# Five weight slots at a stride of 8224 bytes in place of 8192, on a three-part transformer stack

## The reference

```python
def swiglu(h, w_gu, w_down):
    gate, up = jnp.split(h @ w_gu, 2, axis=-1)      # 1024 -> 2 x 2816
    return (jax.nn.silu(gate) * up) @ w_down        # 2816 -> 1024

x = x + 0.5 * swiglu(rms_norm(x, ffn1_norm[l]), ffn1_w_gu[l], ffn1_w_down[l])
h = rms_norm(x, mix_norm[l]) @ a_w_in[i]
...
x = x + jnp.concatenate([o_a, o_m], axis=-1) @ w_out[l]
x = x + 0.5 * swiglu(rms_norm(x, ffn2_norm[l]), ffn2_w_gu[l], ffn2_w_down[l])
```

## Time and profile before

| | |
|---|---|
| median of 3 runs | 2920.57 us (2917.97 to 2921.03) |
| span of the profiled execution | 2913.7 us |
| TensorE busy | 2827.3 us, 97% |
| VectorE busy | 1796.8 us, 62% |
| ScalarE busy | 1492.0 us, 51% |
| DMA | 489.12 MB, mean 168 GB/s |

### The profile page before, as it was taken

One profiled execution on the slowest core, in us unless ns is written; L12 is line 12 of the kernel. 1 busy time (PEld: TensorE's weight loads), 2 busy tenths in 40 slices (PEclk: granted clock), 3 DMA queues, 4 the chain that ended last, 5 costly groups with the idle time before them and its releaser, 6 DMA issues. The chain is left out here.

```text
span 2913.7 us, 47309 instructions
## 1 busy us (share of the span) xinstructions
PE 2827.3 (97%) x20443; PEld 2624.9 (90%) x20443; DVE 1796.8 (62%) x2467; ACT 1492.0 (51%) x2011; POOL 26.5 (1%) x41
## 2 busy tenths in 40 slices
PE   8999999999998999999999999999999999999999
PEld 7998978999986999999998988989999899998898
DVE  5557756566566656555678655566556655656655
ACT  6447435455455545443575634454454544544643
POOL 1000000000000000000001000000000000000000
PEclk9999999999999999999999999999999999999999
DMA  6555115555552556555452455555555555554553
GB/s 231 184 175 162 52 44 186 187 166 181 188 161 87 179 188 203 190 188 171 138 182 92 145 169 194 188 173 188 188 177 176 170 188 187 182 189 150 196 189 129
DMA packets 370110, 489.12 MB, mean 168 GB/s; under 512 B 15424, under 2 KB 329186, under 8 KB 369776
## 3 DMA queue, kind: packets, MB, share of 16 engines
q1 hardware_dynamic: 368944, 485.90, 51.9%
q0 software_dynamic: 640, 0.20, 0.0%
q10 hardware_dynamic: 320, 0.01, 0.0%
HBM read 485.02 MB, written 1.05 MB: 167 GB/s over the span
## 5 line engine op out<-in xcount | busy, mean ns | idle before, releaser
L873 PE MATMUL work<-input_hi,weights_hi 128*128 128x256 f32 x3424 | 959.5, 280 | 1.8 <-DVE weights_lo L241 1.7
L876 PE MATMUL work<-input_hi,weights_lo 128*128 128x256 f32 x3424 | 956.2, 279 | 0.0
L875 PE MATMUL work<-input_lo,weights_hi 128*128 128x256 f32 x3424 | 955.9, 279 | 0.0
L231 DVE TENSOR_TENSOR weights_lo<-weights_raw,weights_hi 128x2048 fp32r<-128x2048 f32 (+2 forms) x282 | 629.5, 2235 | 320.1 <-ACT weights_hi L211 319.6
L873 PEld LDWEIGHTS work<-input_hi,weights_hi 128*128 128x128 f32 x3424 | 643.6, 188 | 6.8 <-DVE weights_lo L241 2.1
L875 PEld LDWEIGHTS work<-input_lo,weights_hi 128*128 128x128 f32 x3424 | 643.5, 188 | 4.4
L876 PEld LDWEIGHTS work<-input_hi,weights_lo 128*128 128x128 f32 x3424 | 643.5, 188 | 0.0
L215 ACT ACTIVATE weights_hi<-weights_raw,params 128x512 fp32r<-128x512 f32 (+2 forms) x736 | 462.0, 701 | 329.7 <-DMA weights_raw<-in_ffn_w_in 164.0
L211 ACT ACTIVATE weights_hi<-weights_raw 128x2048 fp32r<-128x2048 f32 (+2 forms) x282 | 524.0, 1864 | 169.3 <-DMA weights_raw<-in_ffn_w_up 101.1
L241 DVE SCALAR_TENSOR_TENSOR weights_lo<-weights_raw,params,weights_hi 128x512 fp32r<-128x512 f32 (+2 forms) x736 | 492.6, 733 | 168.6 <-ACT weights_hi L215 168.5
L334 PE MATMUL acc<-weights_hi,hidden_hi 128*128 128x512 f32 x880 | 349.6, 397 | 7.5 <-DVE hidden_lo L1049 5.7
(11 more groups left out here) (565 smaller groups left out, 3462.3 us busy)
## 6 DMA issues: line engine op xcount, KB each, us to landing
weights_raw<-in_ffn_w_gu SPq DMA_DIRECT2D x176, 512.0 KB, 4.7
weights_raw<-in_ffn_w_in SPq DMA_DIRECT2D x176, 512.0 KB, 4.7
weights_raw<-in_ffn_w_down SPq DMA_DIRECT2D x66, 1024.0 KB, 4.9
weights_raw<-in_w_in SPq DMA_DIRECT2D x44, 1024.0 KB, 5.3
weights_raw<-in_ffn_w_out SPq DMA_DIRECT2D x44, 1024.0 KB, 4.9
weights_raw<-in_a_w_in SPq DMA_DIRECT2D x29, 1024.0 KB, 5.5
weights_raw<-in_ffn_w_gate SPq DMA_DIRECT2D x44, 512.0 KB, 3.9
weights_raw<-in_ffn_w_up SPq DMA_DIRECT2D x44, 512.0 KB, 5.0
```

Source lines behind the costliest of these rows:

```text
L231: last = self.nc.vector.tensor_tensor(self.wl[:, n % SLOTS, 0:kc * cols], raw, self.wh[:, n % SLOTS, 0:kc * cols].bitcast(F32), ALU.subtract)
L873: nc.tensor.matmul(o, wh[:, k, ms], K.hi[:, c, :], start=(c == 0 and m == 0), stop=False, skip_group_check=True)
L875: nc.tensor.matmul(o, wh[:, k, ms], K.lo[:, c, :], start=False, stop=False, skip_group_check=True)
L876: last = nc.tensor.matmul(o, wl[:, k, ms], K.hi[:, c, :], start=False, stop=(c == DC - 1), skip_group_check=True)
```

## The change

The slots of the three weight tiles are laid 2056 elements (8224 bytes) apart in place of 2048 (8192 bytes). An item still fills at most 2048 elements of its slot; the last 32 bytes of each slot are not used. `weights_lo` and `weights_hi` grow by 160 bytes each, so `weights_hi` begins 160 bytes later, and every tile behind it 320 bytes later. No instruction is added, removed or moved, and no shape, wait or count is changed.

```diff
@@ -20,6 +20,7 @@
 SLOT = 2048
+STRIDE = SLOT + 8
 SLOTS = 5
@@ -97,9 +98,9 @@
-        self.wl = self.sb("weights_lo", [P, SLOTS, SLOT], F32R)
-        self.raw = nc.alloc_sbuf_tensor_at("weights_raw", [P, SLOTS, SLOT], F32, offset=nc.sbuf_base - SLOTS * SLOT * 4)
-        self.wh = self.sb("weights_hi", [P, SLOTS, SLOT], F32R)
+        self.wl = self.sb("weights_lo", [P, SLOTS, STRIDE], F32R)
+        self.raw = nc.alloc_sbuf_tensor_at("weights_raw", [P, SLOTS, STRIDE], F32, offset=nc.sbuf_base - SLOTS * STRIDE * 4)
+        self.wh = self.sb("weights_hi", [P, SLOTS, STRIDE], F32R)
```

## The result

The changed kernel takes 2927.08 us (median of 11 runs, 2924.39 to 2932.76) against 2917.97 us for the kernel before, measured with it: a ratio of 1.0033, 95% interval 1.0024 to 1.0041. It is slower by a third of a percent: 9.1 us between the two medians, 9.6 us by the ratio. The forecast was 2924 us on a median of 2920.57, slower by 0.1%, with slower as the likeliest of the three signs (0.41).

The account below looks back on a forecast made before the run. TensorE's distance between matmul starts was taken to bound the kernel. Input +6.7 us and hidden -4.0 us sum to +2.7 us on the median of 2920.57, so 2924 us; range 2895 to 2950, the forecast's own 2909 to 2939.

Parts of the forecast that it names:

- The bound: Whole kernel: TensorE, busy 2827.3 of 2913.7 us, sets the time through the distance between starts of two matmuls.
- That addresses count: All matmuls: the streamed operand's start behind the stationary one, modulo 512, sets the distance, 113.4 to 119.9 ns at 256 columns.
- The rival of no effect: All matmuls: addresses don't matter and nothing changes, 2920.6 us; chance 0.20.
- Input, +6.7 us: 13344 matmuls streaming input past weights: mean distance rises from 116.8 to 117.3 ns; bounds -45 to +41 us.
- The signs of being right: Feed-forward stretches: equal counts and waits, distances of 114 to 119 ns repeating every five items, slot 0 quickest, 1 and 2 slowest.
- the pattern is broken: Input matmuls: remainders differing within each group of three slow them, 118.7 ns and 2946 us or 119.9 and 2962; chance 0.18.
- Hidden, -4.0 us: 2640 matmuls of 512 columns, weights past hidden: 231.0 ns, 1.5 ns less each; bounds -14 to +2 us.
- What was left at nothing: Some 2,600 remaining matmuls on weights, rounding, splitting and loads: no change taken.
- The rival that was faster: Matmuls on input and hidden: spreading the slots frees TensorE of collisions, -59 us, 2862 us, or half way 2891; chance 0.13.

Follow-up runs that it names:

- experiments 1 and 2: Kernel before plus a 160-byte gap: first behind weights_hi, 2885.54 us, ratio 0.9896; second ahead of all tiles, 2919.18 us, ratio 1.0005.
- The scans: Kernel before with slots 8224 bytes apart, gaps keeping both weight tiles at equal remainders, input 32 or 192 behind slot 0: single executions 2923.86 and 2924.86 us.
- experiment 5: Kernel before with slots kept at 8192 bytes, 40 unused words ahead of weights_hi and 40 behind it: 2926.64 us, ratio 1.0031.
- experiment 7: in192 plus a gap in each feed-forward placing the hidden tiles at 0 modulo 256 behind the slots: 2903.6 us, ratio 0.9954 to the kernel before.
- in192: Kernel before plus a 160-byte gap behind weights_hi, slots still 8192 bytes apart, input 192 behind both weight tiles: 2885.54 us, ratio 0.9896.
- hid64: in192 plus a gap in each feed-forward placing the hidden tiles at 192 modulo 256 behind the slots: 2878.0 us, ratio 0.9879 to the kernel before.

## Why the prediction was right, and where it was not

**The bound** held. TensorE's start distances set the time; the rest moved by less than 3 us (under "The sum").

**That addresses count** was told as a reading and not as shown. It is shown now: experiments 1 and 2 change one thing each, and the one that moves no tile against another changes nothing. The rival of no effect (0.20) is out. The rule of the Trainium skill's page SBUF — State Buffer, section "Who interferes with whom", that PE never waits on anyone, is about one engine holding up another; as the prediction took it, to say that the place of the operands costs nothing, it does not hold: 113.4 to 120.0 ns for matmuls of one form decide.

**Input, +6.7 us.** The sign was right, the size too small: 118.1 less 116.8 ns on 13344 matmuls is +18 us. Two steps of the pricing were off.

The larger one is the price for what no row had modulo 512. For remainders that are 224, 96, 64, 32 and 0 modulo 256 the prediction took the mean of its six rows, 117.6 ns. The scans show 118.3, 119.9, about 117.5, about 117 and 119.8 ns. It had a row at 352, which is 96 modulo 256, of 119.9 ns, and did not use it because the roles were the other way round; the scans show that this makes no difference. With the measured prices, and still each matmul by its own remainder, slots 0 to 4 come to 115.6, 118.4, 118.1, 119.9 and 117.8 ns, a mean of 117.95: +15 us.

The smaller one is to price each matmul by its own remainder and to average over a group of three. It gave slot 0 as the quickest at 114.8 ns; measured are 117.9, and slots 0, 1, 3 and 4 are alike. Two of three matmuls on slot 0 are at 192, but the third is not, and by experiment 5 the alternation takes the gain away. It costs slot 2 another 1.3 ns, but slot 3, where both remainders are bad ones, is 2.1 ns quicker than its own prices. Over the five slots this nearly cancels, with 3 us left.

The signs of being right came in part: distances that repeat every five items, and slot 2 the slowest, but slot 0 not the quickest and slot 1 not slow. The rival "the pattern is broken" had named the mixing within a group. Its sign, over 118 ns in every slot, did not come: four slots stand at 117.8 or 117.9. Its turning point for more than 0.2%, a mean of 117.5 ns, was passed, and the 118.7 ns of its price was not reached.

**Hidden, -4.0 us.** 232.65 to 231.4 ns on 2640 matmuls is -3.3 us. The size is right, but by luck: the price was a mean of three rows, none at the new remainders, and those that the scans show lie between 227 and 234 ns.

**What was left at nothing.** Attended lost 191 x 5.8 ns = 1.1 us; weights past input and the smaller pairs gained about 1.5 us. Rounding, splitting and loads cost nothing, as said.

**The sum.** 18.0 - 3.3 - 0.4 = +14.3 us. Against it stand 2.8 us less idle time of TensorE (2913.7 - 2827.3 = 86.4 us before, 2923.4 - 2839.8 = 83.6 us after) and the clock: the records of the granted clock hold 24.4 us at the 1.2 GHz level before and 20.3 us after, and half of the difference, 2.0 us, is an estimate of what that saved. That makes +9.5 us against 9.7 us of span. So the forecast of 2924 us beside the measured 2927.08 is closer than its working. It had 3 us of change against 9.1; its median of before was 2.6 us higher than that of the 11 runs; and the 4.8 us that idle time and clock gave back stand in no term of it.

**The rival that was faster** (0.13) had the cause of a gain wrong. Spreading the slots does not help; but the distances it was priced with can be had, if not all at once: one chosen remainder each for input, hidden and attended gave 43 of its 59 us.

## What to carry to other kernels

Where TensorE is the bound, measure the distance between the starts of its matmuls for each pair of tiles and compare it with the columns over the clock: if pairs of one shape differ, move one tile by a few multiples of 32 bytes and measure again. Where a remainder is a good one, keep all operands that take turns in one loop at it, since alternation can undo it (115.6 ns by their own prices, 117.9 measured). And time the whole kernel: a good remainder can be lost by what runs ahead of it. A stride between buffers that is a multiple of 512 is no harm but a help here: it keeps them alike, and one gap then serves all.

## What the runs showed that I had not expected

- The distance between starts of one fp32r matmul ranges from 113.3 to 120.0 ns for 256 columns and from 226.7 to 234.2 ns for 512, at a granted clock of 1.00, by the difference of two addresses modulo 256 and, at some remainders, by the state.
- The remainder that is best for 256 columns (192) is poor for 512 (233.1 ns), and the one that is best for 512 (0, 227.0 ns) is among the worst for 256 (119.8 ns).
- At 192 there are two steady states, 113.3 and 117.8 ns, and the run of matmuls before decides which. In experiment 7 the slower one cost 37 us on input (116.8 ns on average in place of 114.0), and hidden gave 16 us of it back.
- Of the gain in the matmuls a part can be lost again to the clock: in192 has 35.7 us at the 1.2 GHz level in its profiled execution, before 24.4 us, which is 5.6 us of time if TensorE had work in all of it. Other executions differ in this: hid64 has 21.4 us.
- By what means the two addresses make the difference is open. The runs show the dependence, not its mechanism.
